# Value products by token in the attention units of a two-layer decoder step, softmax sums divided out afterwards

## What is computed

```python
# eight heads "n": compressed, selected and window branches, merged by gates
p_s = masked_softmax(s_s ...)                     # branch s: here all earlier keys
o_s = einsum('btgrnp,btgnpd->btgrd', p_s, sel[..., 1, :])
p_w = masked_softmax(s_w ...)                     # branch w: a window of 256 keys
o_w = einsum('btgrl,blgd->btgrd', p_w, kw[:, :, 1])
o_n = gates[..., 0:1] * o_c + gates[..., 1:2] * o_s + gates[..., 2:3] * o_w
# eight heads "d": the top 128 keys by an index score, as a mask on the scores
p_d = masked_softmax(s_d ...)
o_d = einsum('btgrk,btkgd->btgrd', p_d, sel_d[:, :, :, 1])
out = concatenate([o_n, o_d]) @ w_out
def masked_softmax(s, mask):                      # exp(s - max) / max(sum, 1e-30)
```

## Time and profile before

| | us |
|---|---|
| median of 3 runs (1529.03 to 1532.76) | 1531.37 |
| the profiled execution, its own time | 1529.01 |
| its span, first to last instruction | 1527.4 |
| busy PE / DVE / ACT / POOL | 1433.2 / 839.6 / 493.1 / 384.4 |

### The profile page before, as it was taken

How to read it: one execution, slowest core, us unless ns; L and a number is a source line. 1 busy time by engine, 2 the same in 40 slices (tenths; PEclk the granted TensorE clock), 3 DMA queues, 4 the chain that set the end, 5 groups by cost and what they waited for, 6 DMA issues and landing times. The chain is left out here.

```text
span 1527.4 us, 27053 instructions
## 1 busy us (share of the span) xinstructions
PE 1433.2 (94%) x10893; PEld 1316.3 (86%) x10893; DVE 839.6 (55%) x1674; ACT 493.1 (32%) x972; POOL 384.4 (25%) x458
## 2 busy tenths in 40 slices
PE   6999988989999999998888899998989999999996
PEld 5999955989999999997788555665889999999996
DVE  3434977465343333438799868667476334343435
ACT  3322123444031230325311434545445213031221
POOL 3025323553010110147423441001364011010102
PEclk9999999999999999998999999999999999999998
DMA  4522340023223123112243231102131322322301
GB/s 146 159 86 88 87 165 6 9 103 111 69 98 111 63 104 111 58 47 56 83 74 94 62 124 39 56 1 56 56 111 56 111 78 89 111 70 97 111 29 56
DMA packets 87195, 123.82 MB, mean 81 GB/s; under 512 B 24438, under 2 KB 42302, under 8 KB 87040
## 3 DMA queue, kind: packets, MB, share of 16 engines
q1 hardware_dynamic: 82048, 107.00, 21.9%
q0 software_dynamic: 5024, 15.10, 3.3%
HBM read 115.62 MB, written 8.57 MB: 81 GB/s over the span
## 5 line engine op out<-in xcount | busy, mean ns | idle before, releaser
L980 PE MATMUL ps<-xh,ring_lo 128*128 128x260 f32 (+2 forms) x2496 | 505.5, 285 | 1.4 <-ACT big L1480 1.4
L980 PEld LDWEIGHTS ps<-xh,ring_lo 128*128 128x128 f32 (+2 forms) x2496 | 386.0, 189 | 3.3 <-ACT big L1480 2.3
L980 PE MATMUL ps<-xh,wr 128*128 128x260 f32 (+1 forms) x1568 | 356.2, 288 | 18.7 <-POOL xl L777 7.2
L980 PE MATMUL ps<-xl,wr 128*128 128x260 f32 (+1 forms) x1568 | 353.8, 287 | 16.0 <-POOL xl L783 8.6
L980 PEld LDWEIGHTS ps<-xh,wr 128*128 128x128 f32 (+1 forms) x1568 | 259.6, 191 | 23.2 <-issue 12.1
L980 PEld LDWEIGHTS ps<-xl,wr 128*128 128x128 f32 (+1 forms) x1568 | 259.0, 191 | 18.2 <-POOL xl L783 9.4
L1827 DVE TENSOR_TENSOR ring_lo<-ring,wr 128x1024 fp32r<-128x1024 f32 (+1 forms) x152 | 201.5, 1329 | 75.1 <-ACT wr L1480 74.9
L980 PE MATMUL ps<-hh,wr 128*128 128x260 f32 x1024 | 222.1, 283 | 0.0
L980 PE MATMUL ps<-hh,ring_lo 128*128 128x260 f32 x1024 | 221.8, 283 | 0.0
L980 PE MATMUL ps<-hl,wr 128*128 128x260 f32 x1024 | 221.7, 283 | 0.0
L795 POOL TENSOR_TENSOR att<-att 128x520 f32<-128x520 f32 (+1 forms) x80 | 76.3, 954 | 556.7 <-DVE att L1851 515.1
(11 more groups left out here) (343 smaller groups left out, 1648.5 us busy)
## 6 DMA issues: line engine op xcount, KB each, us to landing
ring<-in_w_up SPq DMA_DIRECT2D x16, 2048.0 KB, 8.3
ring<-in_w_down SPq DMA_DIRECT2D x16, 2048.0 KB, 7.8
ring<-in_w_in_e SPq DMA_DIRECT2D x9, 1024.0 KB, 7.1
ring<-in_w_in_e SPq DMA_DIRECT2D x2, 2048.0 KB, 8.7
ring<-in_w_out_e SPq DMA_DIRECT2D x2, 2048.0 KB, 8.9
ring<-in_w_in_o SPq DMA_DIRECT2D x16, 256.0 KB, 4.8
ring<-in_w_out_o SPq DMA_DIRECT2D x8, 512.0 KB, 7.3
cbuf<-in_cache_kv POOLq DMA_DIRECT2D x32, 128.0 KB, 2.3
```

The costliest lines, as they stand in the source:

```text
L980: last = pe.matmul(bank(g, half)[0:width(g), 0:H2], w[:, k, :], x[:, k, cols(half)], start=first, stop=final)
```

## The change

- **Values by token.** The transposed probabilities become the stationary operand (128 x 128) and V moves (64 columns). The output is [tokens x head dims], and the eight heads of one (tile, branch) lie side by side in one bank, `ps5/ps6`: 12 **jobs** instead of 32 accumulators. Branch w's units now follow all of s's instead of alternating by head.
- **Division afterwards.** The sums of a job's eight units go to eight columns of `rsum`. DVE's `job_done(o)`, four steps after its last unit, makes one reciprocal, applies the gate, and multiplies the whole bank (128 x 512) into `otok`; for w it then adds the s result. The per-unit reciprocal, gate and probability scaling are gone.
- **Back to head dims.** `final_step`: per tile, PE turns `otok` (four transposes for d; for n four products with the compressed branch and four with the identity) in `ps4` (the last in `ps7`), and DVE's `final_out` copies 128 x 512 into `ymix`. The steps are listed in FINAL_AT; the last two n tiles are finished behind the loop.
- **exp in place**, on four `Pb` buffers of which `sbb` is no longer apart.
- `otok` lies in the `tm` columns kc, vc, ks and kd, so job 0 waits on `store_c` for the `kv_p` store, and that store counts on `store_c`.
- START is 24 instead of 12; the sample steps reach t = 92. `y_hi` of the d heads comes at t = 94 and 95, the n heads' after all eight finals.

```diff
+FINALS = [(3, "d"), (0, "d"), (2, "d"), (1, "d"), (3, "n"), (0, "n"), (2, "n"), (1, "n")]
+FINAL_AT = [20, 22, 39, 41, 69, 71, 86, 95]
...
+        nmx = [piece(1) for _ in range(4)]
+        rsum = [piece(NH) for _ in range(4)]
+        rrec = [piece(NH) for _ in range(2)]
...
-        Pb = [att[:, 3072 + 512 * i:3584 + 512 * i] for i in range(2)]
-        PTb = [att[:, 4096 + 512 * i:4608 + 512 * i] for i in range(2)]
-        sbb = [att[:, 5120 + 512 * i:5632 + 512 * i] for i in range(2)]
+        Pb = [att[:, 3072 + 512 * i:3584 + 512 * i] for i in range(4)]
+        PTb = [att[:, 5120 + 512 * i:5632 + 512 * i] for i in range(2)]
+        otok = [tm[:, :, P * SLOTS.index(n):P * SLOTS.index(n) + P] for n in ("kc", "vc", "ks", "kd")]
...
-        EVERY, START = 2, 12
+        EVERY, START = 2, 24
...
-                for p in range(NP):
-                    o = 1 + max((x[5] for x in units), default=-1)
-                    for br in branches:
+                for br in branches:
+                    for p in range(NP):
                         for g in range(2):
...
+                    jobs += [(late, br), (early, br)]
...
+            pool.dma_start(kv_p[0, 0].rearrange("(i p) s g d -> p i (s g d)", p=P), tm[:, :, 0:768]).then_inc(sm["store_c"], 16)
...
                     if n0 + st:
                         pe.wait_ge(sm["bt_ev"], n0 + st)
-                    else:
-                        pe.wait_ge(sm["pct_ev"], 1)
+                    if st == 0:
...
+            def unit_values(u):
+                i, p, g, br, k0, o = units[u]
+                if u == first_of[o] and o >= 2:
+                    pe.wait_ge(sm["q_g"], o - 1)
+                pe.wait_ge(sm["q_te"], u + 1)
+                c = P * p + HD * g
+                for b in range(i + 1 - k0):
+                    v = tm[:, k0 + b, P * VS[br] + HD * g:P * VS[br] + HD * g + HD]
+                    last = mm(ps[5 + o % 2][:, c:c + HD], PTb[u % 2][:, P * b:P * b + P], v,
+                              start=(b == 0), stop=(b == i - k0))
+                last.then_inc(sm["q_o"], 1)
+
+            def final_begun(f):
+
+                i, kind = FINALS[f]
+                for p in range(NP):
+                    mm(final_bank(f)[:, P * p:P * p + P], VCb[:, p, :], PcT[:, P * i:P * i + P], start=(p == 0))
+
+            def final_added(f):
+
+                o = final_jobs(f)[-1]
+                pe.wait_ge(sm["q_g"], o + 1)
+                for p in range(NP):
+                    last = mm(final_bank(f)[:, P * p:P * p + P], otok_of(o)[:, p, :], ident[:, :], start=False)
+                last.then_inc(sm["of_mm"], 1)
...
+                        continue
...
+                    if f and f < len(FINALS) - 1:
+                        pe.wait_ge(sm["q_of"], f)
+                        pe.wait_ge(sm["q_g"], final_jobs(f)[0] + 1)
+                        for p in range(NP):
+                            last = tr(ps[4][:, P * p:P * p + P], otok_of(final_jobs(f)[0])[:, p, :], P)
+                        last.then_inc(sm["of_mm"], 1)
+                    else:
+                        if f == QT:
+                            pe.wait_ge(sm["bt_ev"], 12)
+                        if f == QT + 2:
+                            pe.wait_ge(sm["bt_ev"], 16)
+                        if f == QT + 3:
+                            pe.wait_ge(sm["pb_ev"], 7)
+                        final_begun(f)
+                        if f < QT + 2:
+                            final_added(f)
...
+                if 0 <= t - 2 < len(units):
+                    unit_turned(t - 2)
                 if t + 1 < len(units):
                     unit_scores(t + 1)
-                            pe.wait_ge(sm["q_of"], o - 1)
-                        if br != "d":
-                            pe.wait_ge(sm["pct_ev"], 1)
-                            mm(acc[:, 0:P], VCb[:, p, :], PcT[:, P * i:P * i + P], stop=False)
-                    pe.wait_ge(sm["q_te"], u + 1)
-                    for b in range(i + 1 - k0):
-                        v = tm[:, k0 + b, P * VS[br] + HD * g:P * VS[br] + HD * g + HD]
-                        last = mm(acc[HD * g:HD * g + HD, 0:P], v, PTb[u % 2][:, P * b:P * b + P],
-                                  start=(br == "d" and b == 0), stop=(b == i - k0))
-                    last.then_inc(sm["q_o"], 1)
+                if 0 <= t - 3 < len(units):
+                    unit_values(t - 3)
                 compressed_step(t)
+                final_step(t)
                 if t >= START:
                     if (t - START) % EVERY == 0:
                         sample_step((t - START) // EVERY)
                     if (t - START) % EVERY == 1:
                         sample_rest((t - START) // EVERY)
+            for f in (QT + 2, QT + 3):
+                final_added(f)
...
+                    if t == first_of[o] and o >= 4:
+                        act.wait_ge(sm["q_g"], o - 3)
+                    act.activation(Pb[t % 4][:, 0:n], Pb[t % 4][:, 0:n], ACT.Exp, bias=nmx[t % 4],
+                                   accum_out=rsum[o % 4][:, 2 * p + g:2 * p + g + 1]).then_inc(sm["q_e"], 1)
...
                 if EARLY <= t < EARLY + NW:
-                    w_hi(NS1 + t - EARLY, ("q_of", 16))
-                if 4 <= t - EARLY < 4 + NP:
-                    y_hi(NP + t - EARLY - 4, "q_of", SMP_DONE)
+                    w_hi(NS1 + t - EARLY, ("pvs_mm", 2))
+                if 0 <= t - (len(units) - 2) < 2:
+                    for k in range(2):
+                        y_hi(NP + 2 * (t - len(units) + 2) + k, "pb_ev", 7)
             for k in range(NP):
-                y_hi(k, "q_of", (2 * QT - 2) * NP + 2 * k + 2)
+                y_hi(k, "q_of", 2 * QT)
...
+
+
+            def job_done(o):
+
+                r = rrec[o % 2]
+                dve.wait_ge(sm["q_e"], last_of[o] + 1)
+                link(dve.reciprocal(r, rsum[o % 4]))
+                if br == "d":
+                    link(dve.tensor_scalar(r, r, 1e30, None, ALU.min))
+                else:
+                    gate = gt[:, i, :].rearrange("x (g p c) -> x p g c", g=2, p=NP)[:, :, :, 1 if br == "s" else 2]
+                    r3 = r.rearrange("x (p g) -> x p g", p=NP)
+                    link(dve.scalar_tensor_tensor(r3, r3, 1e30, gate, ALU.min, ALU.mult))
+                if o == 0:
+                    dve.wait_ge(sm["store_c"], 16 * 3 * MH + 16)
+                dve.wait_ge(sm["q_o"], last_of[o] + 1)
+                last = dve.tensor_tensor(otok_of(o).rearrange("x p (g e) -> x p g e", g=2),
+                                         ps[5 + o % 2][:, :].rearrange("x (p g e) -> x p g e", p=NP, g=2),
+                                         r.rearrange("x (p g) -> x p g", p=NP).unsqueeze(3).to_broadcast([P, NP, 2, HD]),
+                                         ALU.mult)
+                if br == "w":
+                    link(last)
+                    last = dve.tensor_tensor(otok_of(o), otok_of(o), otok_of(o - 2), ALU.add)
+                last.then_inc(sm["q_g"], 1)
+
+            def final_out(f):
+
+                i, kind = FINALS[f]
+                dve.wait_ge(sm["of_mm"], f + 1)
+                k = NP if kind == "d" else 0
+                dve.tensor_copy(ymix[:, k:k + NP, P * i:P * i + P],
+                                final_bank(f)[:, :].rearrange("x (p q) -> x p q", p=NP)).then_inc(sm["q_of"], 1)
 
             for t in range(len(units) + 4):
                 if t < len(units):
...
-                    dve.scalar_tensor_tensor(sbb[t % 2][:, 0:n], tab, SLOPE[NP * g + p], ps[t % 2][:, 0:n], ALU.mult,
+                    if t >= 4:
+                        dve.wait_ge(sm["q_t"], t - 3)
+                    dve.scalar_tensor_tensor(Pb[t % 4][:, 0:n], tab, SLOPE[NP * g + p], ps[t % 2][:, 0:n], ALU.mult,
                                              ALU.add).then_inc(sm["q_sc"], 1)
-                u = t - 1
-                if 0 <= u < len(units):
-                    dve.wait_ge(sm["q_e"], u + 1)
-                    dve.reciprocal(rrec[u % 2], rsum[u % 2]).then_inc(sm["q_g"], 1)
-                if t < len(units):
                     dve.wait_ge(sm["q_sc"], t + 1)
-                    dve.tensor_reduce(nmx[t % 2], sbb[t % 2][:, 0:n], AX.X, ALU.max, negate=True).then_inc(sm["q_m"], 1)
-                u = t - 1
-                if 0 <= u < len(units):
-                    i, p, g, br, k0, o = units[u]
-                    n = P * (i + 1 - k0)
-                    dve.wait_ge(sm["q_g"], u + 1)
-
-                    c = 3 * (NP * g + p) + (1 if br == "s" else 2)
-                    gate = ones[:, 0:1] if br == "d" else gt[:, i, c:c + 1]
-                    link(dve.scalar_tensor_tensor(rrec[u % 2], rrec[u % 2], 1e30, gate, ALU.min, ALU.mult))
-                    dve.tensor_scalar(Pb[u % 2][:, 0:n], Pb[u % 2][:, 0:n], rrec[u % 2], None, ALU.mult).then_inc(sm["q_n"], 1)
+                    dve.tensor_reduce(nmx[t % 4], Pb[t % 4][:, 0:n], AX.X, ALU.max, negate=True).then_inc(sm["q_m"], 1)
```

(20 more changed lines are left out.)

74 lines of the change are left out of this document (36 added, 38 removed).

## The result

| | before | after |
|---|---|---|
| median of 20 runs each, us | 1530.56 | 1535.99 |
| lowest and highest | 1524.97, 1536.78 | 1531.31, 1539.93 |
| profiled execution, its span | 1529.01, 1527.4 | 1537.72, 1536.0 |
| busy PE / DVE / ACT | 1433.2 / 839.6 / 493.1 | 1433.4 / 801.6 / 493.4 |

The ratio is 1.0035, with a 95% interval of 1.0023 to 1.0046: 5.4 us slower. I had forecast 12.4 us slower. The sign and the range held, the size did not, and terms of opposite sign were each off by more than the result, so it is luck that the total came out inside the range.

The account below looks back on a forecast made before the run. PE was taken to bound the loop. Head dims +1.9, sample steps +5.2, store +1.9, idle time -16.9 + 14.5 and end +5.8 gave +12.4 us on the median 1531.37: forecast 1543.5 us, range 1529.5 to 1555.

Parts of the forecast that it names:

- An average unit ... costs PE about 1.6 us, whatever DVE does: Loop: a unit of 2.4 blocks has a PE price of some 1.6 us, the step's 0.34 us of gaps included.
- Value products on PE: nothing: Value records in the loop: loading 128 stationary columns replaces the shorter stream, between 0 and +1.6 us, taken as 0.
- Rival 1: Value records in the loop cost by moving columns, 0.053 us with 64: -19.4 us, 1524 in all; chance 7%.
- DVE's relief costs nothing and gives little: Loop: net 61 us less DVE work is hidden beside a busy PE; only idle time can turn into speed.
- Idle time: From 893 to 1081 us: 16.9 us recoverable, 14.5 us staying or new, 1.4 of it for late d-head copies.
- sample steps owed: Loop: sample work done early before, three pairs and one set of transposes, now falls later: +5.2 us.
- head dims +1.9: Turning outputs back on PE: 2.4 us for d tiles, 6.1 for n tiles, 6.6 of compressed products removed.
- held until 895: At job 0, DVE waits for the kv_p store, so PE starts unit 21's scores at 895.0, not 893.10: +1.9 us.
- The end: From last values to projection: a serial chain of 7.2 us instead of 1.4, +5.8 us; bounds 5.5 and 9.
- `y_hi` at t = 94 and 95: Loop's last units: four d-head copies move from t = 84 to 87 against the last exps, +1.4 us.
- Output weights: Second half loads only some 8 us before the loop's end, landing after 7.3 us, covered by end and first tiles.
- rival 2: Loop: PE never waits behind 895, so all 14.5 us of kept idling goes: 1529 in all; chance 18%.

Follow-up runs that it names:

- its load alone: Kernel after plus one DVE maximum per unit that nobody reads or waits for: 1545.71 us, ratio 1.0114 to the kernel before.
- half-width kernel: Kernel after with each value record taking only 64 of the 128 P^T columns as stationary side: 1536.44 us, ratio 1.0042 to the kernel before.
- widened kernel: Kernel before with each value record taking both heads' 128 V columns as stationary side, result not the attention's: 1519.05 us, ratio 0.9936.

## Why the prediction was wrong, point by point

- **"An average unit ... costs PE about 1.6 us, whatever DVE does", with "the other 0.34 us are two gaps behind semaphores that were already set"**: this is the step that failed. I took PE's idle gaps as a fixed price of a unit, and the full rows as proof that the price could not fall. The gaps went with the 64-column records: 9.8 us faster with DVE unchanged. Nor was DVE free: its multiplication put back costs 7.6 us, its load alone 12. That PE sets the pace between 930 and 1044 was near the truth for the kernel before (2.2 us of waits for DVE there); what filled the rows was not only work.
- **"Value products on PE: nothing"**: right for the record (the step's 1.16 us fits 0.106 each), wrong for the product, since the gaps around it were not counted to it. Rival 1 priced records by their moving columns; of the three shapes measured only 64 by 64 costs that little, 0.055 us.
- **"DVE's relief costs nothing and gives little"**: the multiplication alone is worth 4.7 us between exp 19 and exp 93 and 7.6 in the total, and 27 us of DVE's busy time left the rows from 893 to 1081 where I had 45. The 61 us net were a sum of durations. In the trace short operations start before the one ahead has ended, so DVE's busy time in the whole program fell by 38.0 us (839.6 to 801.6).
- **Idle time, -16.9 + 13.1 within the loop, and sample steps owed, +5.2**: with head dims +1.9 this made +3.3 for a stretch that measured -15.3. The 18.6 us are the mis-sized part of the sum. "All that a lighter DVE can give back" was counted from PE's idle time alone, so the gaps inside the full rows could not enter it. In the other direction the sum had 2.5 us for a lower clock and the trace has 16 us more at 1.2 GHz than before, which cost perhaps 3 to 5 us (an estimate, from 2.3 and 3.7 us for some 14 us each above). Sample steps, paid early or late, changed the kernel by 1 us (alone) and under 3 (with the store early), not 5.2.
- **The store, "held until 895", +1.9**: right in its mechanism, small by 1.4 us: exp 19 comes 3.3 us later, counted from exp 0. The wait, its place, its cause and the low clock behind it were as said. POOL issued the store 2.4 us later on the clock (889.81 against 887.44), but not later counted from exp 0. What the working left out is that unit 16's values wait for the product too and stand first in PE's queue, at 1.2 GHz (six in 1.54 us). What I had not seen is how cheap the way out is: the store waited behind POOL's product only by program order.
- **The end, +5.8, and `y_hi` at t = 94 and 95, +1.4**: 9.6 and 6.6. The chain was the right one, 1081.1 to 1089.3 is 8.2 us where I had 7.2 for it. Missing were the last sample step in front of exp 94, and PE's fall to 1.2 GHz, which doubled PE's links from 1074 on and reached into the projection.
- **Output weights**: their transfers were issued from 1069.7 us on, and the first read of them is at 1098.1: in time, as said.
- **The range**: rival 2 at 1529.3 lay just outside the 1529.5 that was said to take it in.

Of the rivals, 2 comes nearest to what the loop did, since most of the recoverable time was recovered; the long end hid it in the total.

## What to carry to other kernels

A PE that reads as fully busy may hold gaps: compare its starts with the sum of its records, and look up its weight loads' waits in the same stretch, before taking its time as fixed. Count a gap around a group of records to that group until an edit has shown that it stays. And an end of serial steps costs twice, once in length and once in the clock; independent work put between them (here half of the next contraction) pays for both.

## What the runs showed of the hardware

- With value records of 64 weight columns between records of 128, the weight loads idle 0.33 us behind scores of 256 columns and 0.54 to 0.55 behind scores of 384 (before and in the half-width kernel alike), and 0.17 us behind the values. With 128 columns throughout this idling is gone, and the step takes 1.16 instead of 1.50 us (1.32 where the values move 128 columns too). The widened kernel shows the same 0.33 and 0.55 us in front of sample records with 64 weight rows and 128 columns, whose output covers 128 rows. So an output on half of the rows isn't needed for such a gap; loads of another shape behind scores of 256 or 384 columns had it in the cases read here. At 1.2 GHz it is 1.08 us behind 384 (widened kernel, at 1040.17). The Trainium skill (TensorE: Matmul & The Clock Gate, "The mechanism" in the part on packing small matmuls) says that weight loads run beside records in flight only if their row groups differ, and in the same section that a load into the background weight buffer is pulled ahead as well. Here loads with the same rows do run on behind each other (0.32 us from the scores' loads to the values' in the kernel after, with 0.43 us of scores to stream), if all have 128 columns.
- At the full clock a value record costs 0.055 us with 64 weight and 64 moving columns, 0.103 with 64 and 128; with 128 and 64 the step's sum fits 0.106.
- PE at 1.2 GHz: 10 value records take 2.23 us, 0.22 each, after an idling of 3.20 us; at 2.4 GHz they stand some 0.11 apart.
- With a start flag on a product for columns 128 to 255 of a bank, the first head's compressed part was lost from columns 0 to 127; without that flag, all else the same, it was kept. That fits the next product there overwriting what it should add to. The Trainium skill (PSUM — Partial Sum Buffer, "The four PSUM rules") has this rule for the whole bank, and the two runs of that kernel agree.
